# Attention kernel: the last product with v of a unit is issued behind the first score product of the next unit

## Chip, cores and metric

The kernel is one layer of a hybrid decoder and runs on one core of one Trainium2 chip. The metric is the device time of one execution in microseconds (us). The engines are TensorE (PE; its weight loads are shown apart as PEld), VectorE (DVE), ScalarE (ACT), GpSimd (POOL) and SyncE (SP). Each engine takes its instructions in the order written; engines wait for one another with semaphores.

## The reference, cut to what matters

Input: 2048 tokens of width 1024, float32. The layer runs a norm and an input projection, a state-space branch, differential attention, an output projection, routing and 32 experts, and a last norm. The change lies in the attention alone, which computes for each of 4 heads and each block of 128 query rows:

```python
bias = jnp.where(dist >= 0, -slopes[:, None, None] * dist, -jnp.inf)
scores = jnp.einsum('bhmqd,bhmkd->bhmqk', q_blk, kt).astype(jnp.float32)
scores = scores + bias[None, :, None]
p = jax.nn.softmax(scores, axis=-1)
a = p[:, :, 0] - lam * p[:, :, 1]
return jnp.einsum('bhqk,bhkv->bhqv', a.astype(vt.dtype), vt)
```

There are two softmax maps per head (m = 0, 1), mixed into one, which is then multiplied with v (128 columns per head). An RMS norm per row and head follows.

## The kernel before

`attention` (L1208) works through 64 units, u = 16 * head + i; unit i of a head has one block of 128 query rows and (i + 1) * 128 key columns. The columns are cut into chunks of up to 512, so units 0 to 3 of a head have one chunk and units 12 to 15 have four. A chunk of a unit is called a pair, and pairs are counted through all units.

The work of a unit goes through the engines like this:

- TensorE, `qk` (L1417): the scores of a chunk, two maps of two matmuls each (L1431, L1432), into banks 0 to 3. A pair uses two banks in turn, so a pair's score product waits until VectorE has reduced the pair before the last (`scored`).
- VectorE, `score` (L1306): adds the bias, takes the maximum and writes to `scores` (L1318); after the last chunk the maximum of the row (L1322).
- ScalarE, `exp` (L1359): one exp over the whole width for each map (L1363).
- VectorE, `mix` (L1324): reciprocal of the row sums (L1330), the factor of map 2 (L1332), and the mixed map (L1334).
- TensorE, `turn` (L1434): transposes the mixed map by chunks (L1443) into bank 4 or 5.
- ScalarE, `evacuate` (L1366): copies the transposed chunk to `map_T`, two buffers (L1372).
- TensorE, `pv` (L1447): the product of the transposed map with v, added up over the chunks in bank 6 or 7 (L1458).
- ScalarE, `rows_out` (L1374): reads the finished output out, scaled (L1380), and squares it for the norm (L1383).

The order is written out by hand for each engine. TensorE's iteration n issues the scores of unit n and the transposes and products of unit n - 2, interleaved by chunks: all chunks' `turn`, and `pv` of a chunk one `turn` behind; the last chunk's `pv` ends the iteration. VectorE's iteration n is `score(n)`, then `mix(n - 1)`. ScalarE's iteration n is `exp(n - 1, 0)`, the copies of chunks 0 and 1 of unit n - 2, `exp(n - 1, 1)`, the copies of chunks 2 and 3, then `rows_out(n - 2)`.

A head's output is normalised four units after the head's end (NORM_AT = 20, 36, 52): VectorE's `norm` (L1337, L1344), a square root on ScalarE (`root`, L1387, with a change of its function table), then on TensorE `head_T` (L1462), 16 transposes (L1468) through banks 4 and 5, read out on ScalarE by `finish` (L1393). TensorE issues `head_T` at the end of its iteration n = 21, 37, 53, behind the `pv` of that iteration. SyncE loads q, k and v of the next head (L1250 to L1290) once the score products that used the buffers are done.

Of the kernel before, what the change touches and what calls it, by code (L numbers as in the profile page):

```python
# [1207 lines left out]
def attention(nc, ident, ones, shared, oT, wo, a, d):  # L1208

    UN = HEADS * NT  # L1210
# [3 lines left out]
    chunks_of = lambda u: (u % NT + 1 + GRP - 1) // GRP  # L1214
# [3 lines left out]
    NORM_AT = [(h + 1) * NT + 4 for h in range(HEADS - 1)]  # L1218
    with ExitStack() as ctx:
# [28 lines left out]
        with nc.Block() as block:  # L1248
# [166 lines left out]
            @block.tensor  # L1415
            def _(pe):
                def qk(u, c):  # L1417

                    h, i = u // NT, u % NT
                    if c == 0 and i % GRP == 0:  # L1420
                        if u == 0:
                            pe.wait_ge(shared.first_qk_in, 96)
                        else:
                            pe.wait_ge(qk_in[i // GRP], 96 * (h if i == 0 else h + 1))
                    n = pairs_before[u] + c
                    w = min(BANK, width(u) - c * BANK)
                    if n >= 2:
                        pe.wait_ge(scored, 2 * (n - 1))
                    for m in range(2):
                        qt, out = q_of(i // GRP)[:, m, i % GRP * P:(i % GRP + 1) * P].bitcast(F32R), bank[2 * (n % 2) + m][:, 0:w]  # L1430
                        pe.matmul(out, qt, k_of(4 * h + c, 0)[:, m, 0:w].bitcast(F32R), start=True, stop=False)  # L1431
                        pe.matmul(out, qt, k_of(4 * h + c, 1)[:, m, 0:w].bitcast(F32R), start=False, stop=True).then_inc(qk_done, 1)  # L1432

                def turn(u, c):  # L1434

                    if c == 0:
                        pe.wait_ge(mixed, u + 1)
                    n = pairs_before[u] + c
                    if n >= 2:
                        pe.wait_ge(aT_ready, n - 1)  # L1440
                    w = min(BANK, width(u) - c * BANK) // P
                    for b in range(w):
                        last = pe.transpose(bank[4 + n % 2][:, b * P:(b + 1) * P],  # L1443
                                            S[:, u % SLOTS, 0, c * BANK + b * P:c * BANK + (b + 1) * P], ident[:])
                    last.then_inc(mapT, 1)

                def pv(u, c):  # L1447
                    h, n = u // NT, pairs_before[u] + c
                    w = min(BANK, width(u) - c * BANK) // P
                    pe.wait_ge(aT_ready, n + 1)  # L1450
                    if c == 0 and u % NT == 0:
                        pe.wait_ge(v_in[h % 2], 16 * (h // 2 + 1))
                    if c == 0 and u >= 2:
                        pe.wait_ge(o_used, u - 1)
                        pe.wait_ge(o_sq, u - 1)
                    for b in range(w):
                        kt = GRP * c + b
                        last = pe.matmul(bank[6 + u % 2][:, 0:VD], aT[:, n % 2, b * P:(b + 1) * P], v[h % 2][:, kt],  # L1458
                                         start=kt == 0, stop=kt == u % NT)
                    last.then_inc(pv_chunk, 1)  # L1460

                def head_T(h):  # L1462
                    pe.wait_ge(fin_dve, 3 * (h + 1))
                    for t in range(4):
                        if t >= 2:
                            pe.wait_ge(fin_out, 4 * h + t - 1)
                        for b in range(4):
                            last = pe.transpose(bank[4 + t % 2][:, b * P:(b + 1) * P], o[:, h % 2, 4 * t + b], ident[:])  # L1468
                        last.then_inc(fin_T, 1)
                    pe.wait_ge(fin_out, 4 * h + 4)  # L1470

                for n in range(UN + 2):
                    new = chunks_of(n) if n < UN else 0
                    late = chunks_of(n - 2) if n >= 2 else 0
                    for c in range(min(new, 1)):
                        qk(n, c)
                    for c in range(max(new - 1, late)):
                        if c + 1 < new:
                            qk(n, c + 1)
                        if c < late:  # L1480
                            turn(n - 2, c)
                            if c:
                                pv(n - 2, c - 1)
                    if late:
                        pv(n - 2, late - 1)
                    if n - 1 in NORM_AT:
                        head_T(NORM_AT.index(n - 1))
                head_T(HEADS - 1)


# [865 lines left out]
```

## Time and profile before

| | |
|---|---|
| time, median of 3 runs | 2279.71 us (2276.71 to 2286.16) |
| profiled execution | 2274.78 us |
| its span, first to last instruction | 2273.2 us |
| PE busy | 2026.7 us, 89% of the span |
| PEld busy | 1689.8 us, 74% |
| DVE busy | 1400.1 us, 62% |
| ACT busy | 1078.5 us, 47% |
| POOL busy | 522.9 us, 23% |
| mean granted TensorE clock | 0.950 of full speed |

Busy shares are means over stages that differ; matmuls overlap, and their ends are modelled. In the timeline a row gives the start, the duration, the engine, the line, the operation, output and input, and the count; in brackets stands how long the engine had been idle and what ended that.

### The profile page before, as it was taken

How to read it: one execution, taken by the hardware profiler on the slowest of the kernel's cores; microseconds unless marked ns; L12 is line 12 of the kernel's file. 1: busy time of each engine (PE TensorE's matmuls, PEld its weight loads, DVE VectorE, ACT ScalarE, POOL GpSimd, SP SyncE). 2: the span in 40 equal slices, each digit the busy share in tenths (PEclk: the TensorE clock that was granted, in tenths of full speed). 3: DMA queues.
4: the chain of work that ended last, by engine and by line, in shares of the span. 5: the costliest groups of instructions: out<-in, count | busy, mean ns of one | idle time of the engine just before them, and what ended most of it. 6: DMA issues, size and time to landing. Idle time of an engine off the chain costs nothing. (4 is left out here: it accounts for less than half of the span.)

```text
span 2273.2 us, 32351 instructions
## 1 busy us (share of the span) xinstructions
PE 2026.7 (89%) x10286; PEld 1689.8 (74%) x10287; DVE 1400.1 (62%) x2402; ACT 1078.5 (47%) x1586; POOL 522.9 (23%) x632
## 2 busy tenths in 40 slices
PE   6999999877698989869998399999999999999970
PEld 5888888776587878758887278888888888888860
DVE  4674776457686777754443874585658756455444
ACT  4322211334377777762222264575657656445443
POOL 2000011340000000000000234454445645344340
PEclk9999999898799999989999599999999999999995
DMA  8666977721635233014432497797879978576738
GB/s 263 205 229 215 333 259 228 269 81 57 156 90 121 60 72 74 1 65 134 143 130 102 147 363 247 268 356 228 295 272 372 383 260 302 169 274 203 249 77 311
DMA packets 170682, 458.39 MB, mean 202 GB/s; under 512 B 20496, under 2 KB 69728, under 8 KB 144992
## 3 DMA queue, kind: packets, MB, share of 16 engines
q1 hardware_dynamic: 123616, 285.43, 36.5%
q0 software_dynamic: 30848, 138.24, 19.8%
q10 hardware_dynamic: 16128, 33.56, 4.3%
q8 instruction: 51, 0.84, 0.2%
q14 instruction: 39, 0.32, 0.1%
HBM read 342.08 MB, written 115.10 MB: 201 GB/s over the span
## 5 line engine op out<-in xcount | busy, mean ns | idle before, releaser
L2092 DVE TENSOR_TENSOR w_down_lo<-w_down_raw,w_down_hi 128x2048 fp32r<-128x2048 f32 x64 | 144.0, 2289 | 123.9 <-ACT w_down_hi L2029 123.9
L1318 DVE CUSTOM_DVE_ANT_0 scores<-c_bank,alibi 128x512 f32<-128x512 f32 (+3 forms) x320 | 176.2, 606 | 34.9 <-PE c_bank L1432 34.7
L1458 PE MATMUL c_bank<-v_head,map_T 128*128 128x128 f32 x1088 | 151.8, 285 | 32.3 <-ACT map_T L1372 30.9
L1748 POOL IOTA count_i<- 128x128 int32 x1 | 0.2, 235 | 735.0 <-POOLq L65 735.0
L1458 PEld LDWEIGHTS c_bank<-v_head,map_T 128*128 128x128 f32 x1088 | 135.0, 195 | 44.6 <-ACT map_T L1372 44.0
L2176 PE MATMUL m_bank<-w_down_hi,hidden_T_hi 128*128 128x512 f32 x392 | 159.8, 408 | 6.8 <-DVE w_down_lo L2092 6.8
L2092 DVE TENSOR_TENSOR w_gate_lo<-w_gate_raw,w_gate_hi 128x2048 fp32r<-128x2048 f32 x63 | 141.6, 2289 | 31.2 <-ACT w_gate_hi L2029 30.2
L2155 PE MATMUL m_bank<-w_gate_hi,rows_T_hi 128*128 128x512 f32 x392 | 156.4, 399 | 4.0 <-issue 2.6
L2155 PE MATMUL m_bank<-w_up_hi,rows_T_hi 128*128 128x512 f32 x392 | 159.0, 406 | 0.0
L1363 ACT ACTIVATE scores<-scores,neg_max 128x128 f32<-128x128 f32 (+15 forms) x128 | 153.5, 1199 | 10.6 <-DVE neg_max L1322 10.6
L2156 PE MATMUL m_bank<-w_gate_lo,rows_T_hi 128*128 128x512 f32 x392 | 156.2, 398 | 0.0
L2177 PE MATMUL m_bank<-w_down_lo,hidden_T_hi 128*128 128x512 f32 x392 | 156.2, 398 | 0.0
L2157 PE MATMUL m_bank<-w_gate_hi,rows_T_lo 128*128 128x512 f32 x392 | 155.8, 398 | 0.0
L2092 DVE TENSOR_TENSOR w_up_lo<-w_up_raw,w_up_hi 128x2048 fp32r<-128x2048 f32 x64 | 146.1, 2286 | 15.8 <-ACT w_up_hi L2029 15.8
L2157 PE MATMUL m_bank<-w_up_hi,rows_T_lo 128*128 128x512 f32 x392 | 154.8, 395 | 0.0
L2156 PE MATMUL m_bank<-w_up_lo,rows_T_hi 128*128 128x512 f32 x392 | 154.8, 395 | 0.0
L1431 PE MATMUL c_bank<-k_parts,q_parts 128*128 128x512 f32 (+3 forms) x320 | 125.8, 398 | 12.6 <-DVE max_part L1318 6.8
L2033 ACT ACTIVATE rows_T_hi<-m_bank 128x512 fp32r<-128x512 f32 x100 | 54.5, 596 | 137.7 <-PE m_bank L2148 137.7
L2029 ACT ACTIVATE w_down_hi<-w_down_raw 128x2048 fp32r<-128x2048 f32 x62 | 115.5, 1907 | 7.6 <-DMA w_down_raw<-in_w_down_dram 7.6
L2029 ACT ACTIVATE w_up_hi<-w_up_raw 128x2048 fp32r<-128x2048 f32 x62 | 118.6, 1914 | 0.0
L2044 ACT ACTIVATE rows_out<-m_bank,slot_gate 128x512 f32<-128x512 f32 x98 | 67.5, 689 | 106.2 <-PE m_bank L2181 103.6
L1432 PE MATMUL c_bank<-k_parts,q_parts 128*128 128x512 f32 (+3 forms) x320 | 116.2, 370 | 0.0
(411 smaller groups left out, 5197.0 us busy)
## 6 DMA issues: line engine op xcount, KB each, us to landing
w_gate_raw<-in_w_gate_dram SPq DMA_DIRECT2D x64, 1024.0 KB, 7.7
w_up_raw<-in_w_up_dram SPq DMA_DIRECT2D x64, 1024.0 KB, 8.1
w_down_raw<-in_w_down_dram POOLq DMA_DIRECT2D x64, 1024.0 KB, 8.1
hT_d<-hT_parts SPq DMA_DIRECT2D x32, 512.0 KB, 4.9
hT_parts<-hT_d SPq DMA_DIRECT2D x32, 512.0 KB, 8.2
k_parts<-kT_d SPq DMA_DIRECT2D x64, 256.0 KB, 7.7
u_tok<-in_x_dram SPq DMA_DIRECT2D x16, 512.0 KB, 6.0
qT_d<-qk_out ACTq DMA_DIRECT2D x32, 256.0 KB, 3.6
```

The costliest lines, as they stand in the source:

```text
L1318: dve.tensor_tensor_reduce(S[:, s, m, c * BANK:c * BANK + w], bank[2 * (n % 2) + m][:, 0:w], ramp[:, x0:x0 + w], SLOPES[h], -BIG, ALU.add, ...
L1363: act.activation(S[:, s, m, 0:L], S[:, s, m, 0:L], ACT.Exp, bias=nm[:, s, m:m + 1], accum_out=rs[:, s, m:m + 1]).then_inc(exped, 1)
L1431: pe.matmul(out, qt, k_of(4 * h + c, 0)[:, m, 0:w].bitcast(F32R), start=True, stop=False)
L1432: pe.matmul(out, qt, k_of(4 * h + c, 1)[:, m, 0:w].bitcast(F32R), start=False, stop=True).then_inc(qk_done, 1)
L1458: last = pe.matmul(bank[6 + u % 2][:, 0:VD], aT[:, n % 2, b * P:(b + 1) * P], v[h % 2][:, kt], start=kt == 0, stop=kt == u % NT)
L2029: act.activation(whi[w][:, halves[i]], raw[w][:, halves[i]], ACT.Copy).then_inc(hi_done[w], 1)
L2092: dve.tensor_tensor(wlo[w][:, halves[i]], raw[w][:, halves[i]], whi[w][:, halves[i]], ALU.subtract).then_inc(lo_done[w], 1)
L2155: pe.matmul(to[:], xh[:, k], whi[w][:, c], start=k == 0, stop=False)
L2156: pe.matmul(to[:], xh[:, k], wlo[w][:, c], start=False, stop=False)
L2157: last = pe.matmul(to[:], xl[:, k], whi[w][:, c], start=False, stop=k == KT - 1)
L2176: pe.matmul(DN[h][:], hh[:, k], whi[2][:, part(k)], start=k == 0, stop=False)
L2177: pe.matmul(DN[h][:], hh[:, k], wlo[2][:, part(k)], start=False, stop=False)
```

## The change

In TensorE's order the product of the last chunk of unit n - 3, which ended iteration n - 1, now comes in iteration n, behind the first score chunk of unit n. The head's transposes move with it. The last unit's last product stands behind the loop. No other engine's order changes, and neither do the buffers and semaphores.

```diff
@@ -1474,6 +1474,10 @@
                     late = chunks_of(n - 2) if n >= 2 else 0
                     for c in range(min(new, 1)):
                         qk(n, c)
+                    if n >= 3:
+                        pv(n - 3, chunks_of(n - 3) - 1)
+                        if n - 2 in NORM_AT:
+                            head_T(NORM_AT.index(n - 2))
                     for c in range(max(new - 1, late)):
                         if c + 1 < new:
                             qk(n, c + 1)
@@ -1481,10 +1485,7 @@
                             turn(n - 2, c)
                             if c:
                                 pv(n - 2, c - 1)
-                    if late:
-                        pv(n - 2, late - 1)
-                    if n - 1 in NORM_AT:
-                        head_T(NORM_AT.index(n - 1))
+                pv(UN - 1, chunks_of(UN - 1) - 1)
                 head_T(HEADS - 1)
```

## Rows read from the trace of the kernel before

**Rows 1.** Busy time of each engine in the attention stretch (us, instructions), clock, DMA.
```profile
590.00:1003.00 413.00, 353.33 (x2320) 304.45 (x2320) 305.17 (x930) 294.57 (x631) 0.00 (x0) 0.96 0.32 74
```
**Rows 2.** Waits in the attention stretch: who waited for whom, us in total, times, longest.
```profile
ACT o_head L1380 <- PE c_bank L1458: 44.9, 51, 1.5
...
PE c_bank L1458 <- ACT map_T L1372: 30.9, 40, 3.3
```
**Rows 3.** Timeline, units 4 to 6 of head 0: read-out, exp, copy, product, read-out.
```profile
621.55 0.37 ACT L1380 ACTIVATE o_head<-c_bank,row_inv 128x128 f32<-128x128 f32 x1 [0.45 <-PE c_bank L1458]
...
622.16 1.04 ACT L1363 ACTIVATE scores<-scores,neg_max 128x896 f32<-128x896 f32 x1
...
623.78 0.87 ACT L1372 ACTIVATE map_T<-c_bank 128x512 f32<-128x512 f32 x2 [0.49 <-PE c_bank L1443]
...
624.43 1.60 PE L1458 MATMUL c_bank<-v_head,map_T 128*128 128x128 f32 x12 [0.47 <-ACT map_T L1372]
...
626.13 0.37 ACT L1380 ACTIVATE o_head<-c_bank,row_inv 128x128 f32<-128x128 f32 x1 [0.46 <-PE c_bank L1458]
```
**Rows 4.** Timeline, units 11 to 13 of head 0: one round of the middle units.
```profile
660.43 0.68 DVE L1318 CUSTOM_DVE_ANT_0 scores<-c_bank,alibi 128x512 f32<-128x512 f32 x1
...
661.78 0.19 PEld L1431 LDWEIGHTS c_bank<-k_parts,q_parts 128*128 128x128 f32 x1 [0.16 <-DVE max_part L1318]
...
663.46 0.60 ACT L1372 ACTIVATE map_T<-c_bank 128x512 f32<-128x512 f32 x1 [0.92 <-PE c_bank L1443]
...
665.75 0.17 DVE L1330 RECIPROCAL row_inv<-row_sum 128x2 f32<-128x2 f32 x1 [0.19 <-ACT scores L1363]
...
667.52 0.37 ACT L1380 ACTIVATE o_head<-c_bank,row_inv 128x128 f32<-128x128 f32 x1 [1.31 <-PE c_bank L1458]
```
**Rows 5.** Timeline, wide units 12 to 15 of head 0, TensorE and ScalarE.
```profile
674.02 1.38 PE L1458 MATMUL c_bank<-v_head,map_T 128*128 128x128 f32 x10
...
675.16 0.49 PE L1431 MATMUL c_bank<-k_parts,q_parts 128*128 128x512 f32 x1
675.50 0.37 ACT L1380 ACTIVATE o_head<-c_bank,row_inv 128x128 f32<-128x128 f32 x1 [1.06 <-PE c_bank L1458]
...
676.11 1.91 ACT L1363 ACTIVATE scores<-scores,neg_max 128x1920 f32<-128x1920 f32 x1
...
677.11 0.60 PE L1443 MATMUL c_bank<-ident,scores 128*128 128x128 f32 x4
...
677.99 0.60 ACT L1372 ACTIVATE map_T<-c_bank 128x512 f32<-128x512 f32 x1
...
678.91 1.06 PE L1458 MATMUL c_bank<-v_head,map_T 128*128 128x128 f32 x8
```
**Rows 6.** Timeline, end of head 0: first product and read-out of unit 14.
```profile
687.13 1.16 PE L1458 MATMUL c_bank<-v_head,map_T 128*128 128x128 f32 x8 [1.41 <-ACT map_T L1372]
...
692.01 0.37 ACT L1380 ACTIVATE o_head<-c_bank,row_inv 128x128 f32<-128x128 f32 x1 [1.54 <-PE c_bank L1458]
```
**Rows 7.** Timeline, start of head 1: scores of unit 20, unit 18's last steps.
```profile
704.01 0.68 DVE L1318 CUSTOM_DVE_ANT_0 scores<-c_bank,alibi 128x512 f32<-128x512 f32 x1
...
704.32 0.51 PE L1443 MATMUL c_bank<-ident,scores 128*128 128x128 f32 x3
...
705.41 0.94 PE L1458 MATMUL c_bank<-v_head,map_T 128*128 128x128 f32 x6 [0.58 <-ACT map_T L1372]
...
706.44 0.37 ACT L1380 ACTIVATE o_head<-c_bank,row_inv 128x128 f32<-128x128 f32 x1 [0.39 <-PE c_bank L1458]
```
**Rows 8.** Timeline around the first head's norm and transposes.
```profile
709.00 2.29 DVE L1344 TENSOR_TENSOR o_head<-o_head,o_sumsq 128x2048 f32<-128x2048 f32 x1
...
711.21 0.68 DVE L1318 CUSTOM_DVE_ANT_0 scores<-c_bank,alibi 128x512 f32<-128x512 f32 x1
...
711.46 1.22 PE L1458 MATMUL c_bank<-v_head,map_T 128*128 128x128 f32 x8 [3.27 <-ACT map_T L1372]
...
712.46 3.69 PE L1468 MATMUL c_bank<-ident,o_head 128*128 128x128 f32 x16
```

## The prediction

> **What bounds the kernel now.** I read the busy shares first, then the attention stretch, since the change touches nothing else. It runs from 590 to 1003 us and takes 413 of 2273 us, with TensorE (PE) busy for 353, VectorE (DVE) for 305 and ScalarE (ACT) for 295 [rows 1]. No engine is full, so order and waits decide here. Two waits bear on the moved product. TensorE waits 30.9 us in all for a copied map (L1372) ahead of a product with v (L1458), and ScalarE waits 44.9 us in all for that product before it reads the output out at L1380 (I call that step the read-out) [rows 2]. The first is what the change could give back. The second says who is queued behind it.
>
> Then I read the timeline unit by unit. The four heads repeat nearly alike, and four regimes differ.
>
> Narrow units (two chunks): read-out of unit 4 at 621.55, exp of unit 6 at 622.16, copy of map 5 at 623.78 (ScalarE had waited 0.49 for the transposes), product of unit 5 at 624.43, read-out at 626.13 [rows 3]. TensorE and ScalarE are linked in one loop with only 0.49 of slack on ScalarE.
>
> Middle units (8 to 11): the score reduction begins right behind the mix at 660.43, the third score product waits 0.16 for it at 661.78, the second map copy comes at 663.46 after 0.92 of waiting for TensorE, and the next reciprocal at 665.75 has waited 0.19 for the exp [rows 4]. This loop, mix, reduction, third score product, transposes, second copy, second exp, mix, is closed and doesn't pass through the last product with v at all.
>
> Wide units (12, 13): TensorE runs without a gap, and the first product of the new map starts at 678.91, 0.3 after its copy (677.99 + 0.60) [rows 5]. At the end of a head ScalarE bounds: TensorE waits 1.41 for copies behind long exps, and ScalarE 1.54 for the product [rows 6].
>
> **The change part by part.** No instruction is added or removed. For each of 64 units the last product with v (up to four tiles) swaps places with the next unit's first score product (L1431, L1432). No DMA moves; SP waits on qk_done or on products of a head long finished, and POOL has no work here [rows 1]. Four consequences.
>
> (1) What it gives back: the wait in front of the last product. Only for units of one chunk is that the whole wait. For two chunks and more, the product of the earlier chunk still stands first and still waits for its own copy, as the 0.47 at 624.43 does [rows 3]. Bounds: 0, and 30.9 less three waits of 3.3 at the head changes, which come from ScalarE's queue and not from TensorE's order [rows 2, 8], so 21 us.
>
> (2) What it puts in front of ScalarE. From the score product at 675.16 to the transposes at 677.11 two chunks of 512 columns pass in 1.95, so about 0.95 each [rows 5] (a first chunk has 512 columns in 13 of 16 units). The read-out of each unit comes later by that, less the wait saved. ScalarE keeps its order: behind the read-out stand the next unit's exp, then the copy of the next map, which TensorE needs. Bounds: 0 if each loop has 0.95 of slack; 64 x 0.95 = 61 us if none has. I go regime by regime, with delay = old delay + 0.95 - saved wait - slack.
>
> Units 4 and 5: the read-out of unit 3 comes about 0.6 late (0.95 less a wait like the 0.58 of [rows 7], plus some waiting on DVE). Unit 4's slack I take at 0.4, a little under that of unit 5, so 0.2 is left; unit 4's read-out is then 1.15 late; the slack at unit 5 is 0.49 [rows 3], so 0.7 reaches copy, exp and mix. 0.7 per head, x 4 = 2.8.
>
> Units 6 to 11: the loop through the mix binds [rows 4]. The read-out comes 0.95 late less the wait saved, and the copy that follows has 0.92 to absorb it; TensorE arrives earlier by that wait at the third score product and waits there for DVE that much longer. 0, neither gain nor loss. If that cover were gone, it would cost 0.3 to 0.6 x 6 x 4 = 7 to 14.
>
> Units 12 and 13: the products of chunk 2 end at about 675.0 (674.02 plus eight loads at 0.12), the score product now follows until 675.95, then the last product, and the read-out moves from 675.50 to about 676.35; exp (0.6 later, 1.91 long) and copy (0.60) end at 679.5, where the product started at 678.91: 0.6 [rows 5]. The same step one unit before (read-out of unit 11 some 0.7 late, against about 0.4 of slack, an estimate) brings 0.3: 0.9 per head, x 4 = 3.7.
>
> Units 14 and 15: ScalarE bounds, so each further delay goes through whole. The score product put in front is short there (128 and 256 columns, 0.5 each): 1.0 at three head ends = 3.0 [rows 6]. In the last head no score product follows.
>
> (3) A wait is added in front of the product. The score product needs the bank of two pairs before, so it waits for the DVE reduction (scored), and the product with v, whose operand is there, is stuck behind. In the units at the start of a head that bites. Transposes of unit 18 start at 704.32 and end at about 704.8; the score product of unit 21 would need chunk 0 of unit 20, which DVE reduces from 704.01 to about 705.25 (two maps). So it runs from 705.3 to 706.25 and the product with v, at 705.41 before, begins at 706.25, with the read-out of 706.44 at about 707.3 [rows 7]. Behind it exp, copy, exp and mix follow without slack. Such a delay of 0.75 comes in at unit 15 (a product of four tiles behind 384 columns of scores) and grows by 0.3 to 0.5 a unit up to 18. I take 1.65 per head start, x 3 = 5.0. The first head's start overlaps DVE's work on lambda: 0.
>
> (4) Head change: the head's transposes (L1468) move too. DVE normalises the head from 709.00 and reduces the next scores only from 711.21, so the score product in front can't start before 712.45; the product that began at 711.46 begins at 713.4, the head's transposes at 714.4 instead of 712.46. That is 1.95 later, less 0.95 for the score product already done, and ScalarE's two table changes lie beside it: 0.85 to 1.0, x 3 = 2.6 [rows 8].
>
> Sum: 2.8 + 3.7 + 3.0 + 5.0 + 2.6 = 17 us slower. On the profiled execution (2274.8 us, of it 1.6 outside the span) that is 2292; the three timed runs had a median of 2279.7, 4.9 above it, and would give 2297. I take 2295.
>
> Two rules of the Trainium skill bear on this. For the change: TensorE idles in front of the last product, 30.9 us in all with the earlier ones [rows 2], and Perfetto Trace Analysis, Matmuls, says that independent matmul groups should rotate through PSUM banks so that the evacuation of one overlaps the next group's matmuls. That is what the new order does; by it alone the time falls by consequence (1), a rival below. Against it: PSUM — Partial Sum Buffer, Engine vs sequencer instructions, says that matmuls start and complete in program order, only weight loads being let forward. By it the product can't pass a score product that waits for a bank, as (3) assumes; without it (3) would be 0 and the sum 12. In this trace products also always follow in the order written.
>
> **The rivals.** First, the bubble is filled: TensorE's order bounds and what it saves stays saved. For it speak 353 busy of 413 us [rows 1] and the 0.5 to 0.8 waits at narrow units, which recur 40 times. Against it: at narrow units ScalarE itself had waited for the product (0.46 and 0.39) [rows 3, 7], at middle ones DVE binds [rows 4]. It would give up to 21 us; with half of that given back to DVE's loop about 11 to 15, so 2266 (chance 0.12).
>
> Second, the delays are covered: ScalarE's waits (1.31, 1.06, 1.54 before read-outs) [rows 4 to 6] are slack, the narrow units gain what the wide ones lose. Then the time is 2277 to 2283 (0.31). That the change doesn't do what it says for units of several chunks, where the earlier product's wait stays, ends here too.
>
> Third, the clock: at a head change TensorE already idles 3.27 and its transposes then take 3.69 for 16 [rows 8]. A longer idle could bring the lower level in at more places; 3 to 4 changes at 2 to 3 us more make the sum 25 to 28, so 2304 (0.05).
>
> **How the numbers follow.** The forecast (slower by 8 to 24 us, single 17) has 0.52. A measurement of this kernel tells about 0.5%, 11.4 us, from no change. Part of the forecast's lower end falls inside that: slower 0.55 (the clock case included), same 0.34, faster 0.11. The range goes from the first rival's half gain to the third: 2270 to 2307. The forecast's own range is 2285 to 2303.
>
> **What would show it.** Right: the attention stretch 12 to 22 us longer, the rest unchanged; ScalarE's wait for L1458 well above 44.9; TensorE's wait for L1372 before L1458 not gone but moved to the first product of wide units, and a new wait of TensorE for L1318 at L1431 at head starts; middle units with periods as before. (1) is right if last products show no wait. Wrong: periods of narrow units shorter than 4.58 (626.13 - 621.55) [rows 3], or a wide unit whose first product doesn't wait. That the wide units don't lose would mean my chain from read-out to copy has more slack than read; then the second rival holds.

## The result, and the profile after

The change makes the kernel slower. Seven runs after have a median of 2300.56 us (2294.54 to 2305.32), seven of before 2281.50 us (2271.29 to 2286.16); the ratio is 1.0085, 95% interval 1.0066 to 1.0104. The profiled execution took 2297.28 us, against 2274.78 before: 22.5 more. From the first score product to the last read-out (591.64 to 1001.02 before, 593.17 to 1023.29 after) the attention stretch is 409.38 us before and 430.12 after, 20.7 more. The other 1.8 lie outside it, 1.5 of them ahead of the first score product, where both kernels are the same. I call this stretch "the stretch" below. It varies less between executions than the whole time: in the one kernel that was profiled twice the stretch differs by 3.2 and the whole time by 9.1.

The busy times of the attention after (us, instructions; columns as in [rows 1]), in a window that ends later than that of before:

```profile
590.00:1025.00 435.00, 357.60 (x2322) 306.36 (x2321) 305.21 (x931) 290.96 (x631) 0.00 (x0) 0.94 0.31 72
```

The work is nearly what it was (TensorE 353 before, VectorE 305, ScalarE 295): most of the time went into waits. TensorE's 4 more are no added work, but the same work at a lower mean clock (0.94 against 0.96). The waits of the stretch after, for [rows 2]:

```profile
ACT o_head L1380 <- PE c_bank L1458: 94.5, 62, 4.3
...
PE c_bank L1431 <- DVE max_part L1318: 29.7, 31, 5.3
...
PE c_bank L1458 <- ACT map_T L1372: 18.1, 23, 1.9
...
DVE o_sumsq L1341 <- ACT o_sumsq L1387: 7.0, 3, 2.3
```

TensorE's wait ahead of the product fell from 30.9 to 18.1, as the change says. ScalarE's wait for the product doubled, from 44.9 to 94.5, and a wait of TensorE for VectorE's reduction ahead of a score product (6.8 before) came to 29.7. The last line is VectorE waiting, at the three norms, for the square root on ScalarE (4.0 before).

Timeline after, units 4 to 6 of head 0, for [rows 3]:

```profile
627.59 0.37 ACT L1380 ACTIVATE o_head<-c_bank,row_inv 128x128 f32<-128x128 f32 x1 [1.37 <-PE c_bank L1458]
...
628.20 1.04 ACT L1363 ACTIVATE scores<-scores,neg_max 128x896 f32<-128x896 f32 x1
...
632.49 0.37 ACT L1380 ACTIVATE o_head<-c_bank,row_inv 128x128 f32<-128x128 f32 x1 [1.38 <-PE c_bank L1458]
```

One period is 4.90 (4.58 before), and the read-out waits 1.38 for the product (0.46 before): the next unit's score product, 0.9 long, is in between.

Timeline after, units 11 to 13 of head 0, for [rows 4]:

```profile
667.23 0.19 PEld L1431 LDWEIGHTS c_bank<-k_parts,q_parts 128*128 128x128 f32 x1 [0.51 <-DVE max_part L1318]
...
668.90 0.60 ACT L1372 ACTIVATE map_T<-c_bank 128x512 f32<-128x512 f32 x1 [0.34 <-PE c_bank L1443]
...
671.19 0.17 DVE L1330 RECIPROCAL row_inv<-row_sum 128x2 f32<-128x2 f32 x1 [0.17 <-ACT scores L1363]
```

Before the change the weight load of unit 11's last product waited 0.33 for its copy. The new order saves that wait, and it stands at the third score product of unit 13 now (0.51, 0.16 before); ScalarE's 0.92 of waiting ahead of the copy has shrunk to 0.34. Neither moves the reciprocal: from unit 7 to unit 12 of a head its lateness against before changes by 0.03 at most.

Timeline after, wide units of head 0, for [rows 5]:

```profile
681.97 0.37 ACT L1380 ACTIVATE o_head<-c_bank,row_inv 128x128 f32<-128x128 f32 x1 [1.83 <-PE c_bank L1458]
...
682.58 1.89 ACT L1363 ACTIVATE scores<-scores,neg_max 128x1920 f32<-128x1920 f32 x1
...
684.46 1.07 ACT L1372 ACTIVATE map_T<-c_bank 128x512 f32<-128x512 f32 x2
...
685.10 1.16 PE L1458 MATMUL c_bank<-v_head,map_T 128*128 128x128 f32 x8 [0.43 <-ACT map_T L1372]
```

Read-out, exp and copy follow one another without a gap, and the first product, which started without a wait before, now waits for that copy.

Timeline after, change from head 0 to head 1, for [rows 8]:

```profile
722.16 0.80 PE L1431 MATMUL c_bank<-k_parts,q_parts 128*128 128x512 f32 x1 [5.31 <-DVE max_part L1318]
...
724.03 1.91 PE L1458 MATMUL c_bank<-v_head,map_T 128*128 128x128 f32 x8
725.73 3.35 PE L1468 MATMUL c_bank<-ident,o_head 128*128 128x128 f32 x16
```

TensorE stands 5.31 in front of the score product, with the product (whose map was copied at 720.41) and the head's transposes behind it. The first matmul of the score product and the eight of the product also run longer here: 0.80 and 1.91, against 0.50 and 1.16 at most for the same shapes at the full clock. The granted clock (the last column but two) at the first head change, first before, then after:

```profile
712.00:716.00 4.00, 4.00 (x22) 3.44 (x20) 2.55 (x10) 2.79 (x8) 0.00 (x0) 0.57 0.00 0
716.00:720.00 4.00, 2.65 (x16) 2.05 (x14) 2.20 (x8) 2.49 (x7) 0.00 (x0) 1.00 0.01 2
```
```profile
721.00:727.00 6.00, 4.84 (x18) 4.46 (x19) 4.36 (x16) 1.62 (x6) 0.00 (x0) 0.50 0.00 0
```

The lower level lasts about 7 us at each of the three changes after. Before, it lasts about 7 at the second and 4 at the other two.

And one wait that [rows 7], taken from head 1, could not show, at the start of head 0 (weight loads, then ScalarE's read-out):

```profile
612.75 0.29 PEld L1431 LDWEIGHTS c_bank<-k_parts,q_parts 128*128 128x128 f32 x1 [3.52 <-DMA k_parts<-kT_d]
...
614.20 1.18 PEld L1458 LDWEIGHTS c_bank<-v_head,map_T 128*128 128x128 f32 x4
```
```profile
615.78 0.37 ACT L1380 ACTIVATE o_head<-c_bank,row_inv 128x128 f32<-128x128 f32 x1 [4.30 <-PE c_bank L1458]
```

The score product of unit 4 waits 3.52 for the load of k, with unit 1's product behind it, and ScalarE waits 4.30 for that product. By the code this score product reads q of chunk 1 but k of chunk 0 only; it waits for k of chunk 1 because q and k of a chunk count on one semaphore (`qk_in`).

To place the loss I take the start of each unit's reciprocal (L1330), counted from the first score product, after less before:

```
unit   u   2     3     7    12    14    19    20    21    23    28    30    35    36    37    39    46    51    52    53    60    62    63
after    0.07  3.45  3.91  3.91  4.77  7.06  8.06 10.47 10.80 10.81 11.36 11.58 12.56 13.97 14.30 15.20 16.53 17.52 19.59 19.91 20.76 20.75
```

Nothing is lost between units 7 and 12 of a head; the steps lie at unit 3 of the first head, at the wide units, at head ends, and most of all at head changes (19 to 21, 35 to 37, 51 to 53).

### The profile page after: what moved, and what is told of

Same layout as the page of the kernel before. It is cut to its first block and busy times, and to the rows that moved or that the text cites. A ratio compares the mean times of both kernels' runs of the same rounds, so it can differ in the third digit from the quotient of the medians.

```text
span 2295.7 us, 32351 instructions
## 1 busy us (share of the span) xinstructions
PE 2030.4 (88%) x10286; PEld 1691.6 (74%) x10287; DVE 1401.4 (61%) x2402; ACT 1075.5 (47%) x1586; POOL 522.2 (23%) x632
## 3 DMA queue, kind: packets, MB, share of 16 engines
q0 software_dynamic: 30848, 138.24, 19.6%
## 5 line engine op out<-in xcount | busy, mean ns | idle before, releaser
L1458 PE MATMUL c_bank<-v_head,map_T 128*128 128x128 f32 x1088 | 154.5, 283 | 18.6 <-ACT map_T L1372 18.1
L1431 PE MATMUL c_bank<-k_parts,q_parts 128*128 128x512 f32 (+3 forms) x320 | 133.2, 421 | 38.5 <-DVE max_part L1318 29.7
L1458 PEld LDWEIGHTS c_bank<-v_head,map_T 128*128 128x128 f32 x1088 | 142.2, 196 | 31.5 <-ACT map_T L1372 26.3
L1432 PE MATMUL c_bank<-k_parts,q_parts 128*128 128x512 f32 (+3 forms) x320 | 119.3, 377 | 0.0
```

## Experiments

All were compared with the kernel before on the same chip; a ratio is the whole time over that of the kernel before, with its 95% interval. The stretch comes from one profiled execution each. "Slip" is the reciprocal's lateness as in the table. In the first four and in three of the others, TensorE's loop got a predicate `behind(u)` that says which units' last product follows the next score product:

```diff
+                    if n >= 3 and behind(n - 3):
+                        pv(n - 3, chunks_of(n - 3) - 1)
...
+                    if late and not behind(n - 2):
+                        pv(n - 2, late - 1)
...
```

**Parts of the change.** `behind = u % NT < 4`:

> New order only for units 0 to 3 of each head (one chunk), the head's transposes with them; all other units as before. Measured on the stretch from the first score product to the last read-out, which is 409.4 us before and 430.1 after (+20.7). My theory (a read-out displaced by a score product, plus products stuck behind a score product that waits for VectorE or for a load): +12, of it 3.4 at unit 1 of the first head and about 3 at each of three head changes. Rival (only the stuck products cost, the displaced read-outs are covered by ScalarE's waits): +19 to +21. Rival (filled bubble, the loss lies elsewhere): -2 to -4. Whole time 10 to 14 above the kernel before by mine.

Ratio 1.0041 (1.0025 to 1.0056); stretch 420.5, +11.1. Steps: 4.0 at unit 3 of head 0, then 3.3, 1.7 and 2.4 at the three head changes, and nothing between units 15 and 19. The sum is near what I expected, and both rivals (19 to 21, and -2 to -4) fall.

`behind = 4 <= u % NT < 12`:

> New order only for units 4 to 11 of each head. My theory: the loop through the mix binds, only units 4 and 5 lose what exceeds ScalarE's slack: +1 to +2 us on the stretch, whole time not to be told from the kernel before. Rival (covered read-outs): 0. Rival (filled bubble): -3 to -7, since units 8 to 11 waited 0.28 to 0.59 each before the last product.

Ratio 1.0020 (1.0003 to 1.0036); stretch 416.2, +6.9, much more than expected. Where it goes: 0.56 at unit 3 of head 0, where the order is the old one (a wait of 0.50 for the load of k); 0.33 between units 5 and 6 in each head and 0.36 in all at units 12 to 14, where the order is new; 0 between units 7 and 12. The rest lies where the order is the old one: steps of 1.1 at the ends of heads 0 and 2, of 1.0 and 0.7 between units 20 and 21 and between 52 and 53, and 0.7 behind the last reciprocal. The granted clock shows what those are. Six us at the end of head 0, in this kernel and in the kernel before:

```profile
694.00:700.00 6.00, 6.00 (x42) 6.00 (x41) 2.79 (x4) 3.39 (x6) 0.00 (x0) 0.72 1.04 222
```
```profile
688.00:694.00 6.00, 5.56 (x46) 4.88 (x45) 3.59 (x8) 4.44 (x11) 0.00 (x0) 1.00 1.03 236
...
788.00:794.00 6.00, 6.00 (x43) 6.00 (x43) 3.03 (x4) 3.39 (x7) 0.00 (x0) 0.76 0.96 214
```

In this part's run TensorE is at the lower level for part of every head end, in the kernel before only at head 1's. That is worth 1.1 us at the ends of heads 0 and 2 and 0.7 at that of head 3. At the head changes it is there for about 7 us every time, before only at the second change; that is the 1.0 and 0.7 there, and at the second change the step is 0.03. So about 4.6 of the 6.9 are the clock's and 0.6 the load's, and 1.7 are left for the order itself, as expected. The rival that the filled wait gains 3 to 7 is out.

`behind = u % NT >= 12`:

> New order only for units 12 to 15 of each head. My theory: 0.9 us per head at units 12 and 13 and 1 to 1.5 per head end where ScalarE bounds: +7 to +9 us on the stretch, with a wait of TensorE for the first map copy of unit 13. Rival (covered read-outs): 0 to +1. The three parts together should give 21 us if they don't influence one another.

Ratio 1.0040 (1.0026 to 1.0053); stretch 416.3, +6.9. The first product waits for its copy:

```profile
683.99 1.16 PE L1458 MATMUL c_bank<-v_head,map_T 128*128 128x128 f32 x8 [0.49 <-ACT map_T L1372]
```

Steps: 0.8 between units 12 and 14 in each head; 3.6 is reached by unit 17, of it 1.2 by the lower clock at the end of head 0. The total is just under the 7 to 9 that I expected; the lower clock that the kernel before had at the end of head 1 and at the second head change (1.1 and 1.0) is absent here. The rival of covered read-outs (0 to +1) falls. The three parts add up to 24.9 against 20.7, the surplus being clock and load at unchanged places, most of it in the middle part.

**Unit 1 alone back in the old order** (`behind = u != 1`):

> New order everywhere but at unit 1 of the first head, whose product stands before the score product of unit 4 again. In the changed kernel that score product waited 3.5 us for the load of k with unit 1's product behind it. My theory: the stretch is 3 to 3.5 us shorter than 430.1 (+17 against before), since read-out, exp and mix go on while TensorE waits. Rival (the load just lands late in that run, and TensorE must wait for it in either order): 0 to 1 us shorter, with the wait for the load still about 2 us.

Stretch 426.9, 3.25 shorter than 430.1, which lies in my range, but not for my reason alone. Unit 4's score product now follows unit 1's product without a wait:

```profile
617.76 0.93 PEld L1458 LDWEIGHTS c_bank<-v_head,map_T 128*128 128x128 f32 x4 [1.71 <-ACT map_T L1372]
618.64 0.29 PEld L1431 LDWEIGHTS c_bank<-k_parts,q_parts 128*128 128x128 f32 x1
```

It starts 18.7 behind the first score product (599.94), in the kernel before 18.5 and with the change 19.6. The slip at unit 3 is 1.6 instead of 3.45, so 1.8 of the 3.25 lie where the order differs. Another 1.0 comes at the end of head 0, where the order is the same: the full change had the lower clock there, this run had not (first the change, then this run):

```profile
692.00:698.00 6.00, 4.15 (x25) 4.15 (x25) 1.63 (x3) 4.87 (x7) 0.00 (x0) 0.72 1.06 238
```
```profile
699.00:705.00 6.00, 5.81 (x49) 5.29 (x48) 3.58 (x8) 3.99 (x10) 0.00 (x0) 1.00 1.03 226
```

Of the 1.8, in turn, 0.9 is the load, which landed that much earlier here. In each of the twelve profiled executions, the kernel before included, unit 4's score product starts 0.04 to 0.05 behind the landing of the last packet for chunk 1, which came 18.5 to 20.1 behind the first score product. In the four executions with unit 1 in the new order the slip at unit 3 is the landing less 16.1 (2.4, 2.9, 3.45 and 4.0, for landings at 18.55, 18.98, 19.54 and 20.11). For this run's landing at 18.66 that gives 2.55, an estimate, against the 1.6 measured: setting back unit 1 is worth about 1. The rival of a load that is late by chance, 0 to 1 us, is not refuted by this run. The whole time, ratio 1.0084 (1.0066 to 1.0102), can't tell it from the full change.

**The read-out one step later on ScalarE**, TensorE in the new order:

```diff
                     if n <= UN:
                         exp(n - 1, 0)
+                    if n >= 3:
+                        rows_out(n - 3)
...
-                    if n >= 2:
-                        rows_out(n - 2)
...
+                rows_out(UN - 1)
                 root(HEADS - 1)
```

> The changed kernel, and on ScalarE each unit's read-out also one step later: behind the first exp of the next iteration instead of ahead of it, so that exp and map copy no longer stand behind a read-out that waits for the displaced product. My theory (the displaced read-out is what costs at units 4, 5, 12 to 15 and part of the head starts): the stretch falls from 430.1 to 412 to 419 us, and ScalarE's wait for the product falls from 94.5 to under 15. Rival (only the products stuck behind a waiting score product cost): 426 to 430, since TensorE's order is unchanged.

Ratio 0.9990 (0.9976 to 1.0004); stretch 406.7, so 23.4 less than with the change and 2.6 less than before. ScalarE's wait for the product:

```profile
ACT o_head L1380 <- PE c_bank L1459: 19.2, 19, 3.2
```

With TensorE's order untouched the stretch is back below that of the kernel before, further than I expected, and the rival (426 to 430) is refuted. The wait is 19.2, a little above the 15 that I had named. How much of the 23.4 undoes the change, and how much the late read-out would gain in any order, takes the next run.

**The late read-out with TensorE's old order**:

> The kernel before with TensorE's old order, and only ScalarE's read-out one step later. My theory: ScalarE's wait of 44.9 for the product goes; that shortens only the places where ScalarE bounds (head ends, head starts), so the stretch falls from 409.4 to 402 to 406 us. Rival (those waits are slack everywhere): 409, no change.

Ratio 0.9970 (0.9957 to 0.9983); stretch 399.2, 10.2 less than before, twice the expected. The gain comes in steps of 1.0 to 1.1 at the head ends (unit 15 of each head), 1.1 at units 20, 36 and 52, whose reciprocals stand behind the norm, and 0.3 to 0.4 around. Another 1.1, between units 31 and 32, is the lower clock that the kernel before had there.

So of the 23.4 that the late read-out takes from the changed kernel, 10.2 it takes from the kernel before as well, and 13.2 undo a part of the change. With the late read-out on both sides the new order still costs 7.5 (406.7 against 399.2; medians 2276.8 against 2271.6): 2.8 at unit 3 of the first head, and 1.8, 1.7 and 0.9 between units 20 and 21, 36 and 37, 52 and 53, where a product stands stuck (the first two with more of the lower clock in the new order, the last with the same on both sides).

**Old order at the head changes** (`behind = u + 1 not in NORM_AT`, the read-out as before):

> The changed kernel, but at units 19, 35 and 51 (the ones ahead of the head's transposes) the product and the transposes stand before the next score product again. My theory: TensorE no longer waits 5.5 us for VectorE behind the norm with the product and the transposes stuck; 2.4 to 3 us less at each of three head changes, the stretch 421 to 423 instead of 430.1. Rival (ScalarE's table changes set the time of the head change anyway): 429 to 430.

Ratio 1.0064 (1.0040 to 1.0088); stretch 424.6, 5.5 less than with the change. From unit 19 to 21, 35 to 37 and 51 to 53 the slips grow by 1.2, 0.8 and 1.0 instead of 3.4, 2.4 and 3.1: 1.6 to 2.2 saved each, a little under what I expected. What stays, 1.0 at units 20, 36 and 52, comes from the late read-outs of the units before: the square root stands behind unit 18's read-out in ScalarE's order, and the norm waits for it. The product still waits 4.19 for its copy, but no longer for the reduction, and the head's transposes follow at once:

```profile
719.84 1.77 PE L1458 MATMUL c_bank<-v_head,map_T 128*128 128x128 f32 x8 [4.19 <-ACT map_T L1372]
```

**Late read-out, new order but at unit 1 and the head changes**:

> New order on TensorE but at unit 1 and at units 19, 35 and 51, and the read-out one step later on ScalarE. My theory: both costs gone, what is left is the wait that the new order fills: stretch 399 to 406 us, so 3 to 10 less than before, and as short as or shorter than with the late read-out alone. Rival (the new order has no gain of its own): the same as with the late read-out alone, or longer by up to 3 us.

Ratio 0.9974 (0.9962 to 0.9986); stretch 402.2: 4.6 shorter than with the late read-out and the new order throughout, so the stuck products do cost. It is 3.0 longer than with the late read-out and the old order throughout, 1.7 of it by unit 3 of the first head. That left open whether the new order has any gain of its own.

**Late read-out, new order only for units 4 to 15 of a head**, beside the late read-out with the old order once more:

> The read-out one step later, and TensorE's new order only for units 4 to 15 of each head, where neither a load nor the norm stands in front of the score product. Question: does the new order gain anything once its two costs are taken away? The late read-out with the old order had a stretch of 399.2 us. If the middle loop runs through the mix (my reading) 399 to 400. If the filled wait is worth something in itself: 394 to 397, since units 8 to 11 waited 0.28 to 0.59 each before their last product in every head (6.8 in all).

> The kernel before with only the read-out one step later, once more, on the same chip as the run beside it: the ratio should again be near 0.997 and the stretch 399 to 401 us; if the earlier gain was chance, 1.000.

The first: ratio 0.9960 (0.9946 to 0.9975), stretch 400.8. The second: 0.9963 (0.9951 to 0.9975), stretch 402.4, longer than its 399.2 in the earlier run because of 2.5 at unit 3 of head 0. The two times don't differ. From unit 3 to unit 60 the first gains 7.4, the second 8.5 and the earlier run 9.2. So the new order has no gain of its own, even where nothing stands in its way: the saved wait turns up ahead of the third score product. The weight load of that product at unit 12, first with the new order, then with the old in the earlier run (both with the late read-out):

```profile
655.83 0.19 PEld L1432 LDWEIGHTS c_bank<-k_parts,q_parts 128*128 128x128 f32 x1 [0.80 <-DVE max_part L1318]
```
```profile
655.57 0.19 PEld L1432 LDWEIGHTS c_bank<-k_parts,q_parts 128*128 128x128 f32 x1 [0.37 <-DVE max_part L1318]
```

## Why the prediction was right

It forecast slower by 17 us, 2295 in a range of 2270 to 2307; the median is 2300.6, 19.1 above the kernel before by the medians, and the stretch gives 20.7. Step by step, with the slips of the table:

| term | forecast | measured (steps of the slip) |
|---|---|---|
| units 4 and 5, 4 heads | 2.8 | 1.5 (0.46 + 0.33 + 0.33 + 0.34) |
| units 6 to 11 | 0 | 0 |
| units 12 and 13, 4 heads | 3.7 | 3.2 (0.86 + 0.55 + 0.90 + 0.85) |
| head ends, 3 (units 14 to 19) | 3.0 | 3.8 (2.29 + 0.22 + 1.33) |
| head starts, 3 (step at units 20, 36, 52) | 5.0 | 3.0 (1.00 + 0.98 + 0.99) |
| head changes, 3 (step at units 21, 37, 53) | 2.6 | 5.9 (2.41 + 1.41 + 2.07) |
| start of the first head | 0 | 3.45 |
| sum | 17 | 20.8 |

The direction and the two mechanisms were right. That the sum came so close is partly luck: three terms were too high by 3.9 together (units 4 and 5, units 12 and 13, head starts), three were too low by 7.6, and part of those 7.6 is not the order's.

**The displaced read-out (2)** was right as a mechanism, and it is the larger part of the loss but not all of it: 13.2 of the 20.7 go when the read-out moves too, and 7.5 stay. The loop through exp and copy holds at the wide units (unit 13's first product waits 0 before, 0.43 after), and the middle units hold at 0 through VectorE's loop. The head ends differ only by the clock: the change had 1.0 of it at head 0, the kernel before 1.1 at head 1; head 2, where neither had it, shows the order's own 1.3.

**The stuck product (3, 4)** was right too, but sized wrongly in both places. I booked 1.65 per head start; between units 17 and 19 the reciprocals don't move at all (7.17 and 7.06), because only the read-outs are late. Their lateness is paid one step on, and only once: the square root stands behind unit 18's read-out, and VectorE's norm waits for the root (7.0 for the three norms, 4.0 before), so 1.0 per head. The head changes I had at 0.85 to 1.0. There the run with only the middle units in the new order, whose order at the change is the old one, helps: it too had about 7 us of the lower clock at every change, and its steps are 1.04, 0.03 and 0.69. Less those, the product and the transposes behind the waiting score product cost 1.4 at each change, 4.1 in all, and the clock 1.8 of the 5.9. Setting the head changes back saved 1.6 to 2.2 each (with the read-out as in the change).

**The step that failed** is "The first head's start overlaps DVE's work on lambda: 0". It cost 3.45 in the profiled execution. I had said "No DMA moves", which is true, but not asked which DMA the moved score product waits for. In the kernel before, the score product of unit 4 starts 18.5 us behind the first one with no wait shown; but the load's last packet lands only 0.05 ahead of it. In the new order TensorE is free for it at 609.2, 16.1 behind the first, and k of chunk 1, asked for from 600.5 on, behind v and q, lands at 612.7, with unit 1's product stuck behind the score product. SyncE issuing the loads (start, duration; SPq is its sequencer):

```profile
595.60 0.43 SPq L1267 DMA_DIRECT2D v_head<-v_d  x1
596.39 4.06 SPq L1259 DMA_DIRECT2D q_parts<-qT_d  x2
600.51 3.24 SPq L1264 DMA_DIRECT2D k_parts<-kT_d  x4
```

For the landing that the kernel before had (18.5) the relation above gives 2.4, an estimate; the other 1.1 of the 3.45 is a landing 1.1 later, and whether the order or chance delayed it is open. With unit 1 in the old order the slip at unit 3 was 0 to 0.6 in five profiles but 2.5 in one; with unit 1 in the new order 2.4 to 4.0 in four; with unit 1 alone set back 1.6, and 1.9 in the run that also had the head changes back and the late read-out. Loading that k ahead of v, or giving k a semaphore of its own, was not tried. Without the late landing (1.1) and the clock at the head changes (1.8), about 18 of the 20.7 are the order's, an estimate.

**The rivals.** The filled bubble (0.12) fell with the middle part and with the pair of late read-outs: 12.8 us less wait before the product, none of it time. I had also read its case as stronger than it is ("the 0.5 to 0.8 waits at narrow units, which recur 40 times"): of the 40 waits only 24 lie at units of one or two chunks, three of them the 3.3 of the head changes, and the other 21 are 0.37 to 0.71. "Covered delays" (0.31) fell with the wide part. The clock (0.05): the head ends had the lower level in some executions (+1.1 each), and the head changes had it for 7 us instead of 4 in some (+0.7 to +1.0 each), in kernels of either order. With the new order at the changes one to three of them had it (all three after the change), with the old order none to three; whether the longer wait brings it in more often is not shown. It adds 1.8 to this profile and is not the main cause. Of the signs I named, two came only in part. Last products were to show no wait: the 18.1 before products lie at first chunks, but three waits of 0.49 are at units 16, 32 and 48, whose one product is the last as well. And first products of wide units were to wait: those of units 13 to 15 do, unit 12's doesn't (its weight load waits 0.25).

What beats both kernels is the late read-out: 0.9970 and 0.9963 with TensorE's order as it was. With parts of the new order beside it the ratio is 0.9974 and 0.9960, not to be told from that.

## What to carry to other kernels

Filling an engine's wait with other work delays whatever stood behind the wait: before moving an instruction back, ask which engine's queue stops at its result and what that queue does next. Here the cure was on the other engine: take the instruction that waits out of ScalarE's way, and leave TensorE alone. And a moved instruction brings all its waits with it, DMA and bank among them, to everything behind it, above all at the seams (first unit, head change), where the steady loop's slack isn't there.

## What the runs showed that was not expected

TensorE's clock is at the lower level when the stretch begins (0.59 from 585 to 591.6 before, with TensorE busy for 1.87 of 6.6 us), then TensorE idles 10 us while lambda is worked out, and the clock is still low after that. When it comes back differs from run to run. Clock in the last column but two, three us each: the kernel before, the change, and the second run of the late read-out:

```profile
611.00:614.00 3.00, 2.42 (x18) 2.06 (x17) 2.45 (x12) 2.35 (x9) 0.00 (x0) 1.00 1.03 223
```
```profile
615.00:618.00 3.00, 3.00 (x14) 2.81 (x13) 1.32 (x7) 2.22 (x7) 0.00 (x0) 0.50 1.05 240
618.00:621.00 3.00, 2.44 (x17) 2.01 (x17) 2.58 (x8) 1.93 (x8) 0.00 (x0) 0.95 1.08 242
```
```profile
619.00:622.00 3.00, 2.42 (x11) 1.82 (x9) 1.98 (x9) 0.62 (x2) 0.00 (x0) 0.57 1.05 232
```

Counted from the first score product, the clock is back at 2.4 GHz by 19 us before the change and at about 25 after; in the second run of the late read-out, whose TensorE order is the old one, it is still at 1.2 GHz for most of 21 to 24, where the first run of the same kernel was at 2.4 GHz by 19. The load landed 0.95 later in that second run, the score product's weight load waited 0.87 for it, and the slip at unit 3 was 2.5. So a single profile can be off by 2.5 us there, as much as most terms of my sum or more. The lower clock may be a part of the 3.45 at the first head's start too; that was not measured apart.
